# Norms taken block by block with the last down unit, on one core: Sqrt and reciprocal for Ln and Exp, sums of squares on POOL

## The reference

```python
def _rmsnorm(x, g):
    y = x * lax.rsqrt(jnp.mean(x * x, axis=-1, keepdims=True) + EPS)
    return y * g
...
for layer in range(2):
    mod = silu(c) @ ada_w[layer] + ada_b[layer]           # six rows of 1024 for each sequence
    h = _rmsnorm(x, norm_mix_g[layer]) * (1 + mod[1]) + mod[0]
    mix = mixer(h)        # projection, convolution/attention or convolution/spatial gate, output projection
    x = x + mod[2] * mix
    h = _rmsnorm(x, norm_ffn_g[layer]) * (1 + mod[4]) + mod[3]
    gu = h @ ffn_w_gate_up[layer]
    x = x + mod[5] * ((silu(gu[:HID]) * gu[HID:]) @ ffn_w_down[layer])
y = _rmsnorm(x, final_norm_g)
```

## Time and profile before

| | us |
|---|---|
| median of 3 runs | 2751.89 (2747.90 to 2755.22) |
| the profiled execution | 2759.24 |
| its span | 2757.3 |
| PE busy | 2566.7 (93%) |
| DVE busy | 961.0 (35%) |
| ACT busy | 571.7 (21%) |
| POOL busy | 529.4 (19%) |
| mean granted clock of PE | 0.959 of full |

### The profile page before, as it was taken

How to read it: one execution, slowest core, us unless ns; L and a number is a source line. 1 busy time by engine, 2 the same in 40 slices (tenths; PEclk the granted TensorE clock), 3 DMA queues, 4 the chain that set the end, 5 groups by cost and what they waited for, 6 DMA issues and landing times.

```text
span 2757.3 us, 35559 instructions
## 1 busy us (share of the span) xinstructions
PE 2566.7 (93%) x16005; PEld 2429.7 (88%) x16005; DVE 961.0 (35%) x1508; ACT 571.7 (21%) x722; POOL 529.4 (19%) x175
## 2 busy tenths in 40 slices
PE   7898999697799999999999799998899999999996
PEld 4797777456799999999999799998799999999996
DVE  3454555234602222222222622337422222222226
ACT  3312222331411111111111411132311111111112
POOL 1321001101312211222212322211322222222220
PEclk8898999699899999999999899999899999999998
DMA  8112232355012222122222188511011111111101
...
DMA packets 163522, 246.65 MB, mean 89 GB/s; under 512 B 5871, under 2 KB 150677, under 8 KB 162219
## 3 DMA queue, kind: packets, MB, share of 16 engines
...
## 4 chain that ended last, share of the span: by engine, by line
PE 88%; DVE 6%; DMA 2%; ACT 1%; issue 1%; SPq 1%; ACTq 0%; DVEq 0%
PE ps L1818 75%; PE ps L1855 3%; PE ps L1929 2%; PE ps L2024 2%; PE ps L2042 1%; PE ps L1873 1%; DVE nt L1319 1%; DMA cache<-in_cache_b_kv 1%; PE ps L2074 1%; DMA scratch_o<-o_rows 1%; DVE conv_a L1374 1%; PE ps L1937 1%; PE ps L2033 1%; PE ps L1910 1%; PE ps L2063 1%
## 5 line engine op out<-in xcount | busy, mean ns | idle before, releaser
L1661 POOL TENSOR_TENSOR w_lo<-w_raw,w_hi 128x2048 fp32r<-128x2048 f32 x93 | 436.0, 4688 | 1798.1 <-ACT w_hi L864 1798.1
L1818 PE MATMUL ps<-h_hi,w_hi 128*128 128x352 f32 x3024 | 668.0, 329 | 6.1 <-DVE h_lo L1187 3.4
L1818 PE MATMUL ps<-h_hi,w_lo 128*128 128x352 f32 x3024 | 654.9, 324 | 0.0
L1818 PE MATMUL ps<-h_lo,w_hi 128*128 128x352 f32 x3024 | 654.7, 325 | 0.0
L1818 PEld LDWEIGHTS ps<-h_hi,w_hi 128*128 128x128 f32 x3024 | 512.7, 190 | 25.3 <-issue 20.7
L1818 PEld LDWEIGHTS ps<-h_hi,w_lo 128*128 128x128 f32 x3024 | 521.7, 189 | 0.0
L1818 PEld LDWEIGHTS ps<-h_lo,w_hi 128*128 128x128 f32 x3024 | 517.3, 189 | 0.0
L1180 DVE SCALAR_TENSOR_TENSOR x<-ps,mod,x 128x704 f32<-128x704 f32 x448 | 315.5, 746 | 320.5 <-PE ps L1818 320.5
L1227 DVE TENSOR_TENSOR tmp<-ps,tmp 128x1056 f32<-128x1056 f32 x44 | 55.3, 1258 | 729.7 <-PE ps L1818 729.7
L1818 PE MATMUL ps<-mid_hi,w_hi 128*128 128x352 f32 x1248 | 274.3, 328 | 10.0 <-DVE acc_s L1181 7.4
L864 ACT ACTIVATE w_hi<-w_raw 128x2048 fp32r<-128x2048 f32 x93 | 177.7, 1911 | 496.3 <-PE ps L1818 398.2
...
## 6 DMA issues: line engine op xcount, KB each, us to landing
...
cache<-in_cache_b_kv SPq DMA_DIRECT2D x32, 512.0 KB, 5.3
...
```

The source lines that it names most:

```text
L1661: pool.tensor_tensor(w_lo[raw_of[u].slot], w_raw[raw_of[u].slot], w_hi[u % 2].bitcast(F32), ALU.subtract)\
L1818: mm = pe.matmul(big(t)[:, b, 0:BLK], wt, xt[:, k, b * BLK:b * BLK + BLK], start=(k == 0 and n == 0), stop=(k == K - 1 and n == 2))
```

## The change

The last down unit and the norm become one item ("bound"), and both go through the token blocks in the order `ORDER = (2, 0, 1)`, called turns 0, 1 and 2. The 24 pieces (turn, m) of the down unit fill its eight bigs three at a time (`parts`). ACT squares each piece (352 or 320 columns), POOL adds the squares up, 7 adds for each turn. PE makes the mean of turn 0 after big 4, of turn 1 after big 6, and of turn 2 behind the products by h_hi of turn 0 (at the final norm, behind three transposed tiles). ACT does a Sqrt for each turn, DVE a reciprocal, and then scale, shift, high and low parts follow for each turn; the next project goes turn by turn, too. The sample's affine part and low part move from POOL to DVE. With u the last down unit, the weights of unit u+1 (the project that follows) are split at the start of the bound item, those of unit u+2 among the turns. Norm 0 keeps whole squares (ACT) and adds (DVE), and takes its root and all behind it turn by turn, with the split of unit 1 behind turn 0. The output rows go out in the order 6, 7, 8, 0 to 5.

The diff, cut:

```diff
-    norm(0, 0)
+    def into_norm(weights, col, to, **kw):
+
+        last = Item("down", weights=weights, col=col, unit=take("unit"), big=take("big", 8), **kw)
+        items.append(Item("bound", of=last, begins=True, layer=to[0], which=to[1], n=take("norm"),
+                          misc=take("misc", 3), role="norm" if to[0] < 2 else "final"))
+
+    items.append(Item("norm", layer=0, which=0, n=take("norm"), misc=take("misc", 3)))
...
-            if 1 <= g:
+            if g == GROUPS:
+                into_norm("ffn_w_down", g - 1, (layer + 1, 0), layer=layer, gate=5, src="hidden", slot=(g - 1) % 2, j=g - 1)
+            elif g >= 1:
...
+        ORDER = (2, 0, 1)
+        TURN_OF_TILE = {n: 0 if n >= 6 else 1 if n < 2 else 2 for n in range(9)}
...
+        def parts(i):
+
+            return [(j % 3, j // KT, j % KT) for j in range(3 * i, 3 * i + 3)]
+
+        def sums(n, turn, m):
+
+            return 21 * (n - 1) + 7 * turn + m
+
+        def sq_tile(n, turn, m):
+
+            c = (sums(n, turn, m) - 1) % 6
+            return tmp[:, 2, cols(turn)] if m == 0 else \
+                tmp[:, c // 3, BLK * (c % 3):BLK * (c % 3) + cols(turn).stop - cols(turn).start]
...
+            def squares(it, i):
+
+                big_evacuated(act, it.of.big + i)
+                for bank, turn, m in parts(i):
+                    if m and sums(it.n, turn, m) > 6:
+                        act.wait_ge(sq_summed, sums(it.n, turn, m) - 6)
+                    act.activation(sq_tile(it.n, turn, m), x[:, m, cols(turn)], ACT.Square).then_inc(sq_made, 1)
...
+            def root(it, turn):
+
+                q, b = it.misc + turn, ORDER[turn]
+                act.wait_ge(misc_ready, q + 1)
+                act.activation(tmp[:, 3, b * BLK:b * BLK + BLK], misc(q)[:, 0:BLK], ACT.Sqrt, bias=eps[:, 0:1])\
+                    .then_inc(rs_made, 1)
...
-                    evacuate(it.big, ACT.Ln, tmp[:, 3, :], bias=eps[:, 0:1])
-                    big_evacuated(act, it.big)
-                    act.activation(tmp[:, 3, :], tmp[:, 3, :], ACT.Exp, scale=-0.5).then_inc(rs_made, 1)
...
+                        if turn == 0:
+                            split_hi(1)
+                elif it.kind == "bound":
+                    act.activation(warm, eps[:, 0:1], ACT.Sqrt)
+                    if it.of.unit + 1 in unit_end:
+                        split_hi(it.of.unit + 1)
+                    for i in range(8):
+                        squares(it, i)
+                        if i == 4:
+                            root(it, 0)
+                        elif i == 6:
+                            root(it, 1)
+                        if it.role == "norm":
+                            if i == 4:
+                                highs(it, 0, (0, 1))
+                            elif i == 5:
+                                sample_high(it)
+                            elif i == 6:
+                                highs(it, 0, (2, 3))
+                    if it.role == "norm":
+                        highs(it, 0, (4, 5, 6, 7))
+                        root(it, 2)
+                        split_hi(it.of.unit + 2)
+                        highs(it, 1, range(KT))
+                        highs(it, 2, range(KT))
+                    else:
+                        root(it, 2)
+                        for i in range(1, 9, 2):
+                            t, m = it.out + i, OUT_ORDER[i]
...
+                    ins = dve.scalar_tensor_tensor(x[:, m, c], big(t)[:, bank, 0:c.stop - c.start],
+                                                   mod[:, 6 * d.layer + d.gate, m, 0:1], x[:, m, c], ALU.mult, ALU.add)
+                    if ORDER[turn] == 2:
+                        ins = dve.tensor_tensor(acc_s[:, m, :], big(t)[:, bank, LAST:BLK], acc_s[:, m, :], ALU.add)
+                ins.then_inc(big_free[t % 2], 1)
...
+                c = slice(ORDER[turn] * BLK, ORDER[turn] * BLK + BLK)
+                dve.wait_ge(rs_made, 3 * it.n + turn + 1)
+                dve.reciprocal(tmp[:, 3, c], tmp[:, 3, c]).then_inc(left(it.misc + turn), 1)
+                misc_evacuated(dve, it.misc + turn)
...
+            def scaled_and_low(it, turn):
+                for k in range(0, KT, 2):
+                    scaled(it, turn, (k, k + 1))
+                    if k:
+                        lows(it, turn, (k - 2,))
+                lows(it, turn, (KT - 2,))
 
...
+                    scales(it)
+                    for i in range(8):
+                        residual(it, i)
+                        if i == 2:
+                            gate_sample(it)
+                            sample_squares(it)
+                        elif i == 4:
+                            root(it, 0)
+                            dve.wait_ge(scales_made, it.n + 1)
+                            scaled(it, 0, (0, 1))
+                        elif i == 5:
+                            sample_affine(it)
+                            scaled(it, 0, (2, 3))
+                    scaled(it, 0, (4, 5, 6, 7))
+                    if it.n == 3:
+                        dve.wait_ge(vd_stored, 16)
+                    lows(it, 0, (0, 2, 4, 6))
+                    sample_low(it)
+                    big_evacuated(dve, it.of.big + 5)
+                    for turn in (1, 2):
+                        if turn == 2:
+                            big_evacuated(dve, it.of.big + 7)
+                        root(it, turn)
+                        scaled_and_low(it, turn)
...
+                        elif i == 4:
+                            root(it, 0)
+                            finals(0, (0, 1))
+                        elif i == 5:
+                            finals(0, (2, 3, 4))
+                        elif i == 6:
+                            finals(0, (5, 6, 7))
+                    big_evacuated(dve, it.of.big + 5)
+                    root(it, 1)
+                    finals(1, range(KT))
+                    rows_out(0)
+                    big_evacuated(dve, it.of.big + 7)
+                    root(it, 2)
+                    finals(2, range(KT))
...
+                for bank, turn, m in parts(i):
+                    if m:
+                        pool.wait_ge(sq_made, 24 * (it.n - 1) + 8 * turn + m + 1)
+                        if sums(it.n, turn, m) > 1:
+                            pool.wait_ge(sq_summed, sums(it.n, turn, m) - 1)
+                        acc = tmp[:, 2, cols(turn)]
+                        pool.tensor_tensor(acc, acc, sq_tile(it.n, turn, m), ALU.add).then_inc(sq_summed, 1)
...
+                    for turn in range(3):
+                        lows(it, turn, (1, 3, 5, 7))
+                        if turn == 0:
+                            split_lo(1)
+                elif it.kind == "bound":
+                    if it.of.unit + 1 in unit_end:
+                        split_lo(it.of.unit + 1)
+                    for i in range(8):
+                        add_squares(it, i)
+                        if i == 6 and it.role == "norm":
+                            if it.n == 3:
+                                pool.wait_ge(vd_stored, 16)
+                            lows(it, 0, (1, 3))
+                    if it.role == "norm":
+                        lows(it, 0, (5, 7))
+                        lows(it, 1, (1, 3, 5, 7))
+                        split_lo(it.of.unit + 2)
+                        lows(it, 2, (1, 3, 5, 7))
...
+                for turn in range(3):
+                    for k0 in (0, 4):
                         for m in range(2):
-                            for b in range(3):
-                                mm = pe.matmul(big(t + m)[:, b, 0:BLK], halves[s][:, k, m * P:m * P + P],
-                                               xt[:, k, b * BLK:b * BLK + BLK],
-                                               start=(k == 0 and step == 0), stop=(k == KT - 1 and step == 2))
-                            if k == KT - 1 and step == 2:
+                            if turn == 0 and k0 == 0:
+                                big_slot(t + m)
+                            for k in range(k0, k0 + 4):
+                                if m == 0:
+                                    hi_made(pe, n, turn, k)
+                                    if turn == 0 and k == 0:
+                                        pe.wait_ge(xs_hi, n + 1)
+                                products(turn, 0, k, m)
+                                products(turn, 1, k, m)
+                    if turn == 0 and it.kind == "bound":
+                        mean_square(it, 2)
+                    for k in range(KT):
+                        lo_made(pe, n, turn, k)
+                        if turn == 0 and k == 0:
+                            pe.wait_ge(xs_lo, n + 1)
+                        for m in range(2):
+                            mm = products(turn, 2, k, m)
+                            if turn == 2 and k == KT - 1:
                                 mm.then_inc(big_ready, 1)
...
```

(11 more changed lines are left out.)

370 lines of the change are left out of this document (200 added, 170 removed).

## The result

The changed kernel takes **2768.95 us**, median of 4 runs (2762.73 to 2773.57), against 2751.79 for the kernel before on the same chip: a ratio of **1.0053**, 95% interval 1.0037 to 1.0069, so 10 to 19 us more, 15 by the ratio, which is the figure used below (the two medians alone differ by 17). That is slower, and clear of the 0.3% that the prediction counts as no change. It lies inside the range of the forecast, on rival B's figure of 2769, and not where the forecast itself stood.

The account below looks back on a forecast made before the run. PE, 88% of the chain, was taken as the bound, with time won only where it idles at the norms. Norms 1 to 3 -4.8, norm 0 +3.2, end +1.1 gave -0.5, so 2751.4 us; range 2735 to 2772.

Parts of the forecast that it names:

- rival B: POOL's 352-column instructions have a hidden fixed part, 1.02 us each: +18 us over the norms, 2769; chance 0.20.
- the sample work: 256-column sample operations, 0.4 to 0.5 us each, taken as free within the 0.5 of hand-overs.
- the squares' 21 adds on POOL: Norms 1 to 3: 15.9 us hidden under the down's matmuls, except the last three adds.
- The port: Two-input DVE and POOL instructions exclude each other for whole instructions; turn 0 alternates holds of 0.34 and 0.75 us.
- The reciprocal: DVE, each turn: 2.28 us at 352 columns, from the 32-column row; lower end 0.5.
- The clock: Stretches at 1.2 GHz add 1.2 us at the end of each of norms 0 to 3.
- POOL's add: On POOL, 0.77 us for 352 columns, 0.70 for 320, with no fixed part.
- The queue: Before mean 1, ACT's highs wait for DVE's reciprocal and scaled, delaying square 7 of turn 1; PE stands 4.1 us.
- Norm 0: First norm, from sums ready to the next unit: 44.4 us against 41.2, so +3.2.
- The end: From the last down unit's start to the span's end: 62.6 us against 61.5, so +1.1.
- Rival A: PE keeps full clock, reciprocal costs 1.5: -9 us, 2742, chance 0.23; without port lock between short instructions 2721, chance 0.07.
- Rival C: Reciprocal costs 2.9 us or more at each of five norms: +7, 2758; chance 0.17, half of it slower.

Follow-up runs that it names:

- smalladd: Changed kernel with POOL adding only 16 columns of each square instead of 320 or 352; ratio 0.9965 to the kernel before.
- best0: Changed kernel with adds and low parts on DVE, reciprocal 0 late, split halves beside reciprocals, final mean 2 ahead of transposes; ratio 0.9996 to the kernel before.
- norecip: Changed kernel with all but one column of each reciprocal left out; ratio 0.9946 to the kernel before.
- late: Changed kernel with reciprocal 0 and first scaled tiles behind big 5's residual, ACT's first high parts behind its squares; ratio 1.0026 to the kernel before.

## Why the prediction was right or wrong

The forecast was no change, -0.5 us, and the change costs 15: wrong. The lock, the stall and the queues were mostly seen. The step that failed is the one that put POOL's adds and the sample work at nothing: "the squares' 21 adds on POOL (15.9 us) hide under the down's matmuls but for the last three". They do not hide: taken out but for 16 columns (smalladd) they give back 7.2, 6.7 and 4.8 at norms 1 to 3, where the three that the sum charged are 2.3, and 5.5 at the end. (1.5 of that in norm 2 is a part of the stall, which the sum did have.) Beside that, the low clock was charged at the end of the sum and not at the stall, and one queue was followed wrongly. Norm 2 by the prediction's own steps, in us from the down's start:

| | forecast | measured |
|---|---|---|
| mean 0 ends | 15.2 | 15.3 |
| root 0 | 19.0 | 19.6 |
| last add of turn 1 | 25.6 | 26.9 |
| down ends | 29.1 | 32.2 |
| last residual | 30.7 | 33.8 |
| turn 0 done | 40.3 | 42.3 |
| reciprocal 1 | 42.6 | 44.6 |
| turn 1, with POOL's last low | 51.1 | 53.9 |
| split of unit u+2 | 55.9 | 58.5 |
| turn 2 | 63.4 | 67.6 |
| next unit | 68.8 | 72.1 |

**Right.** The port: behind the down DVE and POOL alternate at 1.09 us a pair (POOL's starts at 1545.97 and 1547.06), which is the 0.34 and 0.75 of the working; turn 0 took 8.5 for 9.6. The reciprocal: 2.34 against 2.28, worked out from 32 columns. The split: 4.59, with DVE behind it. Root, squares and highs on ACT: 0.54, 0.47 to 0.59. That PE would stand some 4 us ahead of tile 7: 4.37, though for POOL's sum and not, as its sign had it, for ACT's root. (A few steps of the working are off by 0.1 to 0.5 us: 51.1 and 4.5 make 55.6, the 21 adds make 15.7, and the slope of 0.83 does not follow from the 0.42 and 1.13 beside it, the second of which has a bias. None bears on the result.)

**The clock, 1.2 put at the end of the sum.** It fell where the stall was, on the path: mean 1 and tile 7 together took 5.3 where the working has 3.5 and full clock takes 3.7. Of the 3.1 by which the last residual is late, 1.8 are this, 1.6 of them the clock. It is not sure to follow: over the ten changed kernels tile 7 took 4.3 to 5.8 us in all 15 places with a wait of 4.1 to 4.7 ahead of its mean, in 8 of the 21 with a wait of 2.0 to 3.1, and in none of the 4 with a wait of 1.1 (best0); everywhere else it took 3.3.

**The sample work, priced at nothing**, and **POOL's add, priced at 0.77.** These two go with the queue below, and the three together are the other 1.3; the trace does not divide it. "Within the 0.5 of hand-overs" holds behind the down; at big 2 the three two-input operations stand among POOL's adds and take 3.1 instead of 1.3, so residual 3, the 1.12 on PE ahead of tile 5, root 0 (by 0.6) and all behind them are late. The add takes 0.94. The 0.50 for 256 columns had been got by taking DVE's hold off POOL's 1.52; the fixed 0.19 would be hidden by that subtraction if it passes while POOL still waits for the port. That fits the 1.09 of a pair, but no run shows it by itself.

**Rival B** had 0.20, and its 2769 is the measured time. That the two agree to the microsecond is luck. It had the price (0.25 fixed, 0.19 measured, with which its own sum is some 14 and not 18) but only half the place: it charged the sixteen POOL instructions behind the down, and there the pair took the forecast 1.09; by the order of instructions in the trace (no run isolates it) the price works ahead of mean 1 and in turns 1 and 2, where DVE has two or three instructions for each of POOL's and POOL comes to a free port. Its "decides once an add takes more than about 0.9" was met.

**The queue.** The prediction had square 7 of turn 1 held by ACT's highs. In the trace it waits for DVE's residual of big 5, which stands behind reciprocal 0 and two scaled tiles; so reciprocal 0 is on the path to mean 1, as the sum had it, though by another queue (norecip: mean 1 2.2 earlier). late moves both and halves the stall; then POOL's rate, an add every 1.09, is what is left.

**Turns 1 and 2**, 8.5 and 7.5, took 9.3 and 9.1; the tail of PE 4.5 to the next unit, where 4.2 and the clock's 1.2 stood. **Norm 0**, 45.7 for 44.4: the first scaled tile waited for the DMA of the bias (`rel_stored`) until 5.9, where the working had it at 4.3. **The end**, 65.8 for 62.6: the down ends at 32.6 for 29 to 30, and that goes through whole. Together: 10.9 at norms 1 to 3 (3.0 of them the wrong first row of norm 1, which the kernel before has too), 1.3, 3.2. Less that row it is 12.4 over the forecast, so 12 over the first trace of before.

**Rival A** had no part in it: PE did not keep its clock, and the port binds for 352 columns (a scaled tile of 352 columns 1.25 to 1.27 beside a POOL low, 0.58 alone). The Trainium skill ("SBUF — State Buffer", Who interferes with whom) calls the shared pair an exclusive lock from which a DVE instruction with at most one SBUF input is free. Both halves of that show here, in the 3.81 beside the split and in the reciprocal's 2.33 beside 2.40 of it. (The 3.43 against 1.28 that the prediction gives for it bears on the lock alone.) **Rival C**: by the Trainium skill's repeat count of 8 ("VectorE: DVE Perf Modes", First, the fixed hardware budget) a reciprocal would have been 2.93, an estimate. Every one took 2.34 to 2.36, so the row of 32 columns was the better guide.

**The range** held the time because it was drawn out to B. The chances did not deserve to stand as they did: POOL's add, the sample work and the clock each stood at or near its lower bound in the sum, and three such terms on one path are not a likeliest case.

What stays open: no kernel ran with only norm 0 or only the end undone, so how the 15 us divide among them is read from traces alone; Ln and Exp turn by turn was not tried; no run has the adds at another length than 16 columns, so how much of their price is the hold of the port and how much POOL's rate ahead of mean 1 is not divided; and what decides whether tile 7 keeps the full clock behind a wait of 2 to 3 us is not known.
